# First two blocks on shared x tiles, the sums inside the token projections, the fourth block's low weights on VectorE, and the meta tokens' operations ahead of the chunk operations

## The chip, the cores and the metric

One NeuronCore of one Trainium2 chip runs the whole program. The metric is device time in microseconds; the kernel before takes 1088.43 us (median of three runs, 1088.21 to 1089.88).

## The reference

One decoder layer over 528 tokens: 16 learned meta tokens ahead of 512 real ones, model width 1024. Eight heads of width 128 run a gated delta rule; a short gated convolution runs beside it; both are merged by sigmoid gates, projected, and followed by a SwiGLU network of width 2816 and a last RMSNorm.

```
xn = rms_norm(h, norm1)
q, k, v, z, b_raw, a_raw, sc_c, sc_u, sc_b, gate_a, gate_b = split_columns(xn @ w_in, PROJ_WIDTHS)
q, k, v = silu(causal_depthwise_conv(q, k, v)), q and k L2-normalised per head
beta = sigmoid(b_raw);  g = -exp(a_log) * softplus(a_raw + dt_bias)
o = chunk_gated_delta_rule(q, k, v, g, beta)    # the meta tokens form their own first partial chunk
y_a = (rms_norm(o, o_norm) * silu(z)) @ w_dn_out
y_b = (sc_b * causal_depthwise_conv(sc_c * sc_u, conv_sc)) @ w_sc_out
h = h + (sigmoid(gate_a) * y_a + sigmoid(gate_b) * y_b) @ w_o
gt, up = split(rms_norm(h, norm2) @ w_gate_up)
h = h + (silu(gt) * up) @ w_down;  return rms_norm(h, final_norm)[:, 16:]
```

In each chunk the delta rule solves a triangular system (a_mat + I); the kernel inverts that matrix level by level, blocks of 1, 2, 4 up to 64, for the four chunks of 128 real tokens (am, tm, um) and in small for the chunk of 16 meta tokens (ma, mt, mu).

## The kernel before, in words

**Blocks.** All matrix products are cut into blocks of 128 output channels. The list BLOCKS holds for each head q, k, v, z, c, u, b, then the gates and output projections, then the SwiGLU network; block n is the n-th of the list, counted from 0. A block is eight tiles k of 128 input channels. Each weight block is 512 KB, comes by DMA on SP's queue into one of three slots of w_raw, and is split in two parts whose products are exact enough together: the high part w_hi (ScalarE, split_weights, half a block at a time, counted by whi_ready) and the low part w_lo, the difference (POOL, split_weights, counted by wlo_ready; for the first three blocks VectorE, first_low_weights, counted by wlo_first). x is split the same way (x_hi on ScalarE in plain_high, x_lo on VectorE in plain_low). Every tile then takes three products on TensorE: w_hi x_hi, w_hi x_lo, w_lo x_hi; a block over 528 or 516 tokens does each in two halves (big[n % 2]).

**The start.** first_blocks does blocks 0 and 1 (q and k of head 0) in two passes: a high pass with x_hi, block after block, and a low pass with x_lo. Meanwhile ScalarE squares the x tiles (square), VectorE adds them (add_square), and TensorE sums them over partitions with a matrix of ones; from that ScalarE makes the inverse root rs1, by which the results of all projections are scaled later. Then come token_projections (beta and decay inputs, 32 matmuls into dbank[0:2], signalled by bat_done), whose copy is turned inside block 2 (turn_token_projections), token_sums behind block 2, and turn_decays in block 3. token_factors and token_decays are the ScalarE and VectorE sides of these. ScalarE's functions Silu and Exp/Ln lie in different tables, and changing between them is an instruction of its own (ACT_TABLE_LOAD).

**Order on each engine.** Every engine runs its own list in program order, written out by hand: a loop over blocks n and quarters q of a block. In it each engine takes one step of the generator delta_steps (from block 4 on, four steps a block, 28 steps a head, so steps 0 to 3 of a head lie in its block b and steps 4 to 7 in the next head's block q), a piece of evacuate for the block before, and a weight split. TensorE takes a step after every second tile. An engine that waits holds all that stands behind it in its list.

**Steps 0 to 4 of a head.** TensorE, step 0: the products k k^T into dbank[1] (kk_done). VectorE, step 0: am, the two operations on tm, the transpose into um (u_ready). POOL, step 0: level_mask(0), then in block b both halves of the next block's low weights. VectorE, step 1: the meta operations bv, bk, ma, mkdec, mvb (ma_ready, mkv_ready), which need TensorE's mpre_done and ScalarE's mx_ready and km_root (L564). POOL, step 1: mt and the three malev (mt_ready). ScalarE, step 3: the product of level 0 copied into pb, then dbank[2] cleared (cleared), after mkv_ready. TensorE, step 3: level 0 with um and alev (L1024, um,alev). TensorE, step 4:

```
pe.wait_ge(pb_ready, done + 1)
if l == 0:
    pe.wait_ge(mt_ready, h + 1)
    if h:
        pe.wait_ge(o_root, h)
    mm(dbank[0][0:META, 0:META], mt[:, :], ident[0:META, 0:META]).then_inc(mt_turned, 1)
    pe.wait_ge(mkv_ready, h + 1)
...
if l == 0:
    pe.wait_ge(cleared, h + 1)
```

Of the kernel before, what the change touches and what calls it, by code (L numbers as in the profile page):

```python
# [65 lines left out]
def hybrid_block_kernel(nc, h_t, w_stream, w_ba, small, consts, out):  # L66
# [5 lines left out]
    with ctx:  # L72
# [196 lines left out]
        def wait_low(engine, n, half):  # L269
            if n < 3:  # L270
                engine.wait_ge(wlo_first, 2 * n + half + 1)
            else:
                engine.wait_ge(wlo_ready, 2 * (n - 3) + half + 1)
# [5 lines left out]
        def _(sp):  # L279
            sp.dma_start(sm[:, :], small[:, :]).then_inc(small_in, 16)  # L280
            for part in range(4):
                sp.dma_start(h_in[:, 2 * part:2 * part + 2, :], h_t[:, 2 * part:2 * part + 2, :]).then_inc(h_loaded[part], 16)
                if part == 0:
                    sp.dma_start(w_raw[:, 0, :], w_stream[0, :, :]).then_inc(w_in[0], 16)
            for n in range(1, STREAM):
# [20 lines left out]
        def _(pool):  # L306
# [25 lines left out]
            def delta_steps():  # L332
                for h in range(-1, HEADS + 1):
                    for step in range(0 if h >= 0 else PRE, STEPS if h < HEADS else TRAIL):
# [7 lines left out]
                        if step == 0:  # L342
                            pool.wait_ge(a_ready, h + 1)
                            level_mask(0)
                        if step == 1:
# [5 lines left out]
                            ins.then_inc(mt_ready, 1)  # L351
                        if step == 2:
# [26 lines left out]
            for n in range(STREAM + 1):  # L379
                weights_first = n < MAIN and BLOCKS[n][0] == "b"  # L380
                for q in range(4):
# [5 lines left out]
                    if q in (1, 2) and 3 <= n + 1 < STREAM and not weights_first:  # L387
# [18 lines left out]
        def _(act):  # L406
# [30 lines left out]
            split_weights(0, 0)  # L437
            split_weights(0, 1)
            for k in range(2, KT):
                plain_high(k)  # L440
            split_weights(1, 0)
            split_weights(1, 1)
            for k in range(KT):
                square(k)
            act.wait_ge(ba_in, 16)
            copy(wba_hl[:, :, 0:16], wba[:, :].rearrange("p (k c) -> p k c", c=16)).then_inc(wba_hi_ready, 1)
            split_weights(2, 0)
# [11 lines left out]
            ins.then_inc(rs1_ready, 1)  # L459
            def token_factors():  # L460
# [41 lines left out]
            def delta_steps():  # L502
                for h in range(-1, HEADS + 1):
                    nxt = h + 1
                    for step in range(0 if h >= 0 else PRE, STEPS if h < HEADS else TRAIL):
# [32 lines left out]
                        if step == 3:  # L538
# [48 lines left out]
            def evacuate(n, kind, m):  # L587
                p = big[n % 2]
                act.wait_ge(block_done, n + 1)
                if kind == "z":  # L590
# [43 lines left out]
            for n in range(STREAM + 1):  # L634
                chores = evacuate(n - 1, *BLOCKS[n - 1]) if 1 <= n <= MAIN else iter(())
                for q in range(4):
# [10 lines left out]
                    if q in (1, 2) and 3 <= n + 1 < STREAM and not weights_first and not weights_at_once:  # L647
                        split_weights(n + 1, q - 1)
                    if q == 3 and n == 2:
                        token_factors()  # L650
                    if q == (0 if n > 3 else 3) and 2 <= n and n - 2 < MAIN and BLOCKS[n - 2][0] in ("q", "k", "v"):
                        silu(*BLOCKS[n - 2])
                    if q == (0 if n < AT["gb", 0] else 2) and n in EXP_LN_FROM:
                        nc.scalar.preload_act_table_set("natural_log_exp_and_others")
                if n == 2:
# [24 lines left out]
        def _(dve):  # L680
# [26 lines left out]
            for k in range(5):  # L707
                plain_low(k)
            first_low_weights(1)
            for k in range(5, KT):  # L710
                plain_low(k)
            for k in range(1, KT):
# [3 lines left out]
                                    wba_hl[:, :, 0:16].bitcast(f32), ALU.subtract).then_inc(wba_ready, 1)  # L716
# [639 lines left out]
```

## Time and profile before

| what | value |
|---|---|
| median of the runs | 1088.43 us (1088.21, 1088.43, 1089.88) |
| profiled execution | 1087.92 us, span of its trace 1086.1 us |
| granted TensorE clock, mean | 0.995 of full speed |
| TensorE busy | 1063.2 us, 98% of the span |
| VectorE, ScalarE, POOL busy | 417.1, 423.3, 553.6 us |
| DMA | 95.44 MB, mean 88 GB/s |

The span runs from the first to the last instruction of the profiled execution; the time of that execution is 1.8 us longer. PE is TensorE's matmuls, PEld its weight loads, DVE VectorE, ACT ScalarE. A bracket behind a row tells how long the engine stood idle before it and what ended that; "issue" means that the profile shows no releaser. L1024 is the helper through which TensorE issues all its matmuls.

### The profile page before, as it was taken

What the parts mean: (1) busy time and instruction counts of PE and PEld (TensorE: products, weight loads), DVE (VectorE), ACT (ScalarE), POOL (GpSimd) and SP (SyncE); (2) the same over time, 40 slices, a digit from 0 to 9 for tenths busy, and PEclk for the clock granted to TensorE, in tenths of its full rate; (3) what the DMA queues carried; (4) which work ended last, traced back from release to release, by engine and by line L of the source; (5) the groups of instructions that cost most, each with busy time, mean ns of one, the idle gap of its engine ahead of it and who ended that gap; (6) DMA issues with size and microseconds to landing.
All of it is one profiled execution on the core that took longest, in us unless ns stands there. A gap on an engine that the chain in (4) does not pass through costs nothing.

```text
span 1086.1 us, 20289 instructions
## 1 busy us (share of the span) xinstructions
PE 1063.2 (98%) x8233; PEld 906.8 (83%) x8233; DVE 417.1 (38%) x772; ACT 423.3 (39%) x950; POOL 553.6 (51%) x471
## 2 busy tenths in 40 slices
PE   8999999999999999999999999999999999999997
PEld 8989898989898898978888888878888888888886
DVE  6665756657575657553211212212111121200001
ACT  6726354453545353533322233443322333332222
POOL 1263635364544535363545565655555555554553
PEclk9999999999999999999999999999999999999999
DMA  6221212121212121211432222222322223222222
GB/s 221 73 84 62 70 61 85 63 69 60 89 60 83 58 77 60 78 60 60 129 142 97 97 91 88 93 97 97 97 97 85 90 97 97 98 97 97 95 80 78
DMA packets 28812, 95.44 MB, mean 88 GB/s; under 512 B 2984, under 2 KB 5288, under 8 KB 28720
## 3 DMA queue, kind: packets, MB, share of 16 engines
q1 hardware_dynamic: 27520, 91.77, 25.4%
q10 hardware_dynamic: 1200, 2.38, 0.6%
q8 instruction: 65, 1.06, 0.4%
q14 instruction: 27, 0.22, 0.1%
HBM read 92.03 MB, written 2.11 MB: 87 GB/s over the span
## 4 chain that ended last, share of the span: by engine, by line
PE 96%; DVE 1%; issue 1%; ACT 1%; DMA 1%; POOL 0%; SPq 0%; DVEq 0%
PE bank L1024 95%; DMA h_in<-h_t 1%; DVE qkv L704 0%; ACT x_hi L422 0%; PE bank L1216 0%; PE bank L1222 0%; DVE x_lo L690 0%; DVE w_lo L698 0%; POOL mt L313 0%; DVE tm L767 0%; DVE h L1015 0%; PE bank L1229 0%; PE bank L1228 0%; DVE cv L929 0%; DVE am L687 0%
## 5 line engine op out<-in xcount | busy, mean ns | idle before, releaser
L326 POOL TENSOR_TENSOR w_lo<-w_raw,w_hi 128x512 fp32r<-128x512 f32 x316 | 415.6, 1332 | 477.5 <-ACT w_hi L413 476.4
L1024 PE MATMUL bank<-x_hi,w_hi 128*128 128x258 f32 (+2 forms) x896 | 249.0, 336 | 0.6 <-DVE w_lo L698 0.6
L1024 PE MATMUL bank<-x_hi,w_lo 128*128 128x258 f32 (+2 forms) x896 | 231.0, 316 | 0.0
L1024 PE MATMUL bank<-x_lo,w_hi 128*128 128x258 f32 (+2 forms) x896 | 228.9, 316 | 0.0
L413 ACT ACTIVATE w_hi<-w_raw 128x512 fp32r<-128x512 f32 x322 | 187.5, 618 | 92.3 <-PE bank L1024 92.2
L1024 PE MATMUL bank<-og_hi,w_hi 128*128 128x512 f32 x416 | 164.7, 396 | 0.0
L1024 PE MATMUL bank<-og_hi,w_lo 128*128 128x512 f32 x416 | 164.3, 395 | 0.0
L1024 PE MATMUL bank<-og_lo,w_hi 128*128 128x512 f32 x416 | 164.3, 395 | 0.0
L1024 PEld LDWEIGHTS bank<-x_hi,w_lo 128*128 128x128 f32 x896 | 148.2, 190 | 11.3
L1024 PEld LDWEIGHTS bank<-x_hi,w_hi 128*128 128x128 f32 x896 | 146.9, 190 | 12.8 <-DVE w_lo L698 0.8
L1024 PEld LDWEIGHTS bank<-x_lo,w_hi 128*128 128x128 f32 x896 | 147.2, 190 | 8.9
L1024 PEld LDWEIGHTS bank<-og_hi,w_hi 128*128 128x128 f32 x416 | 78.0, 187 | 19.2 <-issue 0.2
L1024 PEld LDWEIGHTS bank<-og_lo,w_hi 128*128 128x128 f32 x416 | 78.0, 187 | 19.2 <-issue 0.2
L1024 PEld LDWEIGHTS bank<-og_hi,w_lo 128*128 128x128 f32 x416 | 78.0, 187 | 19.2
L858 DVE SCALAR_TENSOR_TENSOR cv<-raw,sm,cv 128x528 f32<-128x528 f32 (+1 forms) x72 | 72.2, 1002 | 1.5
L1024 PE MATMUL bank<-f_hi,w_hi 128*128 128x512 f32 (+1 forms) x182 | 68.9, 378 | 0.0
L1024 PE MATMUL bank<-f_hi,w_lo 128*128 128x512 f32 (+1 forms) x182 | 68.7, 377 | 0.0
L1024 PE MATMUL bank<-f_lo,w_hi 128*128 128x512 f32 (+1 forms) x182 | 68.6, 377 | 0.0
L687 DVE TENSOR_TENSOR tg<-bank,rs 128x512 f32<-128x512 f32 x22 | 15.2, 692 | 110.1 <-PE bank L1024 101.7
L1024 PE MATMUL bank<-yb_hi,w_hi 128*128 128x512 f32 x128 | 51.6, 403 | 0.0
L1024 PE MATMUL bank<-yb_lo,w_hi 128*128 128x512 f32 x128 | 50.5, 395 | 0.0
L1024 PE MATMUL bank<-yb_hi,w_lo 128*128 128x512 f32 x128 | 50.5, 395 | 0.0
(261 smaller groups left out, 1300.5 us busy)
## 6 DMA issues: line engine op xcount, KB each, us to landing
w_raw<-w_stream SPq DMA_DIRECT2D x162, 512.0 KB, 3.3
h_in<-h_t SPq DMA_DIRECT2D x4, 528.0 KB, 5.9
h<-h_t ACTq DMA_DIRECT2D x1, 2048.0 KB, 10.9
h_in<-gc_dram SPq DMA_DIRECT2D x7, 264.0 KB, 3.1
out<-h SPq DMA_DIRECT2D x4, 256.0 KB, 2.9
out<-h SPq DMA_DIRECT2D x2, 384.0 KB, 2.6
cst<-consts SPq DMA_DIRECT2D x1, 512.0 KB, 8.3
h_in<-gc_dram ACTq DMA_DIRECT2D x1, 264.0 KB, 3.0
```

The lines of the kernel that those rows point to most:

```text
L326: nc.gpsimd.tensor_tensor(low_weights(n)[:, at], w_raw[:, n % 3, at], high_weights(n)[:, at].bitcast(f32), ALU.subtract).then_inc(wlo_read ...
L413: return nc.scalar.activation(to, x, ACT.Copy)
L687: return nc.vector.tensor_tensor(to, a, b, ALU.mult)
L858: ins = nc.vector.scalar_tensor_tensor(to, xj, taps[:, j:j + 1], to, ALU.mult, ALU.add)
L1024: return nc.tensor.matmul(o, w, x, start=start, stop=stop)
```

## The change

- SP asks for the second block's weights ahead of the second part of x; ScalarE and VectorE split them ahead of x tiles 2 to 7.
- The high pass of the first two blocks runs tile by tile, both blocks on each, after tiles 0 and 1 of the first and then of the second.
- ScalarE and VectorE handle four squares, then wba, then the other four; TensorE's sums of squares move from before the token projections to the middle of them.
- Block 3's low weights go from POOL to VectorE, its high ones ahead of the third block on ScalarE. In head 0 the last tap of the convolutions of q, k and v (a scaled copy of raw) goes from VectorE to ScalarE's evacuate, token_factors on ScalarE from the end of the third block's loop round to the end of the second's, and VectorE copies the token projections ahead of the first convolution.
- Per head, VectorE's and POOL's meta operations go from step 1 to the front of step 0, and ScalarE's clear of dbank[2] from step 3 to step 1.

```diff
--- before.py
+++ after.py
@@ -267,10 +267,10 @@
         def wait_low(engine, n, half):
-            if n < 3:
+            if n < 4:
                 engine.wait_ge(wlo_first, 2 * n + half + 1)
             else:
-                engine.wait_ge(wlo_ready, 2 * (n - 3) + half + 1)
+                engine.wait_ge(wlo_ready, 2 * (n - 4) + half + 1)
         def wait_gate_used(engine, i):
@@ -281,8 +281,9 @@
                 if part == 0:
-                    sp.dma_start(w_raw[:, 0, :], w_stream[0, :, :]).then_inc(w_in[0], 16)
-            for n in range(1, STREAM):
+                    for n in range(2):
+                        sp.dma_start(w_raw[:, n, :], w_stream[n, :, :]).then_inc(w_in[n], 16)
+            for n in range(2, STREAM):
                 if n == 2:
@@ -340,15 +341,14 @@
                         if step == 0:
-                            pool.wait_ge(a_ready, h + 1)
-                            level_mask(0)
-                        if step == 1:
                             pool.wait_ge(ma_ready, h + 1)
...
                             ins.then_inc(mt_ready, 1)
+                            pool.wait_ge(a_ready, h + 1)
+                            level_mask(0)
                         if step == 2:
@@ -384,7 +384,7 @@
                         next(delta, None)
-                    if q in (1, 2) and 3 <= n + 1 < STREAM and not weights_first:
+                    if q in (1, 2) and 4 <= n + 1 < STREAM and not weights_first:
                         split_weights(n + 1, q - 1)
@@ -434,16 +434,17 @@
             plain_high(1)
-            split_weights(0, 0)
-            split_weights(0, 1)
+            for n in range(2):
+                split_weights(n, 0)
+                split_weights(n, 1)
             for k in range(2, KT):
                 plain_high(k)
-            split_weights(1, 0)
-            split_weights(1, 1)
-            for k in range(KT):
+            for k in range(4):
                 square(k)
...
             copy(wba_hl[:, :, 0:16], wba[:, :].rearrange("p (k c) -> p k c", c=16)).then_inc(wba_hi_ready, 1)
+            for k in range(4, KT):
+                square(k)
             split_weights(2, 0)
@@ -457,6 +458,8 @@
             ins.then_inc(rs1_ready, 1)
+            split_weights(3, 0)
+            split_weights(3, 1)
             def token_factors():
@@ -535,7 +538,7 @@
                             ins.then_inc(pb_ready, 1)
-                        if step == 3:
+                        if step == 1:
                             act.wait_ge(mkv_ready, h + 1)
@@ -587,6 +590,12 @@
                 act.wait_ge(block_done, n + 1)
+                if kind in ("q", "k", "v") and m == 0:
+                    i = ("q", "k", "v").index(kind)
+                    c, first, last = conv_number(kind, 0), META if kind == "q" else 0, CQKV + 4 * 8 * i + 3
+                    act.wait_ge(raw_scaled, i + 1)
+                    nc.scalar.activation(cv[:, c % 2, first:], raw[:, c % 2, 3 + first:], ACT.Copy,
+                                         scale=sm[:, last:last + 1]).then_inc(raw_ready, 1)
                 if kind == "z":
@@ -644,14 +653,14 @@
                     next(chores, None)
-                    if q in (1, 2) and 3 <= n + 1 < STREAM and not weights_first and not weights_at_once:
+                    if q in (1, 2) and 4 <= n + 1 < STREAM and not weights_first and not weights_at_once:
                         split_weights(n + 1, q - 1)
-                    if q == 3 and n == 2:
-                        token_factors()
                     if q == (0 if n > 3 else 3) and 2 <= n and n - 2 < MAIN and BLOCKS[n - 2][0] in ("q", "k", "v"):
...
                         nc.scalar.preload_act_table_set("natural_log_exp_and_others")
+                if n == 1:
+                    token_factors()
                 if n == 2:
@@ -704,16 +713,16 @@
             first_low_weights(0)
-            for k in range(5):
+            first_low_weights(1)
+            for k in range(KT):
                 plain_low(k)
-            first_low_weights(1)
-            for k in range(5, KT):
-                plain_low(k)
-            for k in range(1, KT):
+            for k in range(1, 4):
                 add_square(k)
...
                                     wba_hl[:, :, 0:16].bitcast(f32), ALU.subtract).then_inc(wba_ready, 1)
+            for k in range(4, KT):
+                add_square(k)
             link(nc.vector.tensor_scalar(on_scaled[:, :], sm[:, ONORM:ONORM + 1], float(128) ** 0.5, None, ALU.mult))
@@ -757,17 +766,6 @@
                         if step == 0:
-                            dve.wait_ge(kk_done, h + 1)
-                            dve.wait_ge(xb_ready, h + 1)
-                            mult(flat(am), dbank[1][:, :], flat(am)).then_inc(a_ready, 1)
-                            dve.wait_ge(a_ready, h + 1)
-                            dve.wait_ge(tm_set, h + 1)
-                            t = cols4(tm[:, :, :], 1, 0)
-                            link(mult(t, cols4(am[:, :, :], 1, 0), const_cols(cst[:, CLEV, :], 1, 0)))
-                            nc.vector.tensor_tensor(t, const_cols(ident, 1, 0), t, ALU.subtract).then_inc(t_ready, 1)
-                            dve.wait_ge(t_ready, h + 1)
-                            nc.vector.transpose(flat(um), flat(tm)).then_inc(u_ready, 1)
-                        if step == 1:
                             dve.wait_ge(mpre_done, h + 1)
@@ -779,6 +777,16 @@
                                                     ALU.mult).then_inc(mkv_ready, 1)
+                            dve.wait_ge(kk_done, h + 1)
+                            dve.wait_ge(xb_ready, h + 1)
+                            mult(flat(am), dbank[1][:, :], flat(am)).then_inc(a_ready, 1)
+                            dve.wait_ge(a_ready, h + 1)
+                            dve.wait_ge(tm_set, h + 1)
+                            t = cols4(tm[:, :, :], 1, 0)
+                            link(mult(t, cols4(am[:, :, :], 1, 0), const_cols(cst[:, CLEV, :], 1, 0)))
+                            nc.vector.tensor_tensor(t, const_cols(ident, 1, 0), t, ALU.subtract).then_inc(t_ready, 1)
+                            dve.wait_ge(t_ready, h + 1)
+                            nc.vector.transpose(flat(um), flat(tm)).then_inc(u_ready, 1)
                         if step == 11:
@@ -880,22 +888,15 @@
                     if c == 0:
-                        nc.vector.tensor_scalar(cv[:, 0, META:], raw[:, 0, 3 + META:], sm[:, last:last + 1], None,
-                                                ALU.mult).then_inc(raw_ready, 1)
-                        dve.wait_ge(raw_ready, 1)
-                        taps = convolve(0, META, sm[:, CQKV + 4 * m:CQKV + 4 * m + 4])
-                        next(taps)
                         dve.wait_ge(bat_done, 1)
                         for s in range(2):
-                            ins = mult(bat[:, s * HALF:(s + 1) * HALF], dbank[s][0:32, 0:HALF],
-                                       rs1[0:32, s * HALF:(s + 1) * HALF])
+                            ins = mult(bat[:, s * HALF:(s + 1) * HALF], dbank[s][0:32, 0:HALF], rs1[0:32, s * HALF:(s + 1) * HALF])
                         ins.then_inc(bat_copied, 1)
-                        yield
-                        yield from taps
-                        return
+                        first_low_weights(3)
                     first = META if kind == "q" else 0
-                    nc.vector.tensor_scalar(cv[:, c % 2, first:], raw[:, c % 2, 3 + first:], sm[:, last:last + 1], None,
-                                            ALU.mult).then_inc(raw_ready, 1)
+                    if m:
+                        nc.vector.tensor_scalar(cv[:, c % 2, first:], raw[:, c % 2, 3 + first:], sm[:, last:last + 1], None,
+                                                ALU.mult).then_inc(raw_ready, 1)
                     dve.wait_ge(raw_ready, 3 * m + i + 1)
@@ -1036,15 +1037,14 @@
                     return parts, [big[n][s][:, 0:part.stop - part.start] for s, part in enumerate(parts)]
-                for n in range(2):
+                for k, n in [(0, 0), (1, 0), (0, 1), (1, 1)] + [(k, n) for k in range(2, KT) for n in range(2)]:
                     parts, to = outs(n)
-                    for k in range(KT):
-                        if k % 4 == 0:
-                            wait_low(pe, n, k // 4)
-                        pe.wait_ge(xhi_ready, k + 1)
-                        for w in (w_hi, w_lo):
-                            for o, s in zip(to, parts):
-                                mm(o, w[:, n, k * 128:(k + 1) * 128], x_hi[:, k, s], start=k == 0 and w is w_hi, stop=False)
+                    if k % 4 == 0:
+                        wait_low(pe, n, k // 4)
+                    pe.wait_ge(xhi_ready, k + 1)
+                    for w in (w_hi, w_lo):
+                        for o, s in zip(to, parts):
+                            mm(o, w[:, n, k * 128:(k + 1) * 128], x_hi[:, k, s], start=k == 0 and w is w_hi, stop=False)
                 for n in range(2):
@@ -1052,6 +1052,7 @@
                     ins.then_inc(block_done, 1)
+            def x_square_sums():
                 pe.wait_ge(x_added, KT - 1)
@@ -1063,6 +1064,8 @@
                                      start=k == 0 and rows == 32, stop=k == KT - 1 and rows == 32)
+                    if k == KT // 2 - 1:
+                        x_square_sums()
                 ins.then_inc(bat_done, 1)
...
```

## Rows read from the trace of the kernel before

**Rows 1.** The page: busy us, share of the span, instructions.
```profile
PE 1063.2 (98%) x8233; PEld 906.8 (83%) x8233; DVE 417.1 (38%) x772; ACT 423.3 (39%) x950; POOL 553.6 (51%) x471
```

**Rows 2.** TensorE's waits: total us, times, longest.
```profile
PE bank L1024 <- issue: 10.6, 8, 1.5
...
PE bank L1024 <- POOL malev L313: 1.4, 1, 1.4
```

**Rows 3.** All engines in order of time, second head, 112 to 122 us.
```profile
112.02 0.19 ACT L564 ACTIVATE h_in<-h_in 16x1 f32<-16x1 f32 x1
...
113.46 0.69 DVE L687 TENSOR_TENSOR am<-bank,am 128x512 f32<-128x512 f32 x1 [1.43 <-PE bank L1024]
...
114.23 1.09 POOL L313 TENSOR_TENSOR alev<-am,cst 128x256 f32<-128x256 f32 x1 [4.15 <-DVE am L687]
...
114.64 0.96 DVE L767 TENSOR_TENSOR tm<-cst,tm 128x256 f32<-128x256 f32 x1
...
115.28 1.49 POOL L326 TENSOR_TENSOR w_lo<-w_raw,w_hi 128x512 fp32r<-128x512 f32 x1
...
115.64 0.71 DVE L769 STREAM_TRANSPOSE um<-tm 128x512 f32<-128x512 f32 x1
...
117.68 0.40 PE L1024 MATMUL bank<-x_hi,w_lo 128*128 128x512 f32 x1
...
118.00 0.44 PE L1024 MATMUL bank<-um,alev 32*32 32x16 f32 x32
...
118.38 0.51 PE L1024 MATMUL bank<-x_hi,w_hi 128*128 128x258 f32 x2
118.52 0.41 ACT L413 ACTIVATE h_in<-bank 128x256 f32<-128x256 f32 x1 [1.33 <-PE bank L1024]
...
118.97 1.18 POOL L313 TENSOR_TENSOR mt<-ma,cst 16x16 f32<-16x16 f32 x1 [0.41 <-DVE ma L777]
119.07 0.33 DVE L780 TENSOR_SCALAR mvb<-bank,h_in 16x128 f32<-16x128 f32 x1
...
119.69 0.40 PE L1024 MATMUL bank<-x_hi,w_lo 128*128 128x258 f32 x2
...
120.89 0.57 POOL L313 TENSOR_TENSOR malev<-ma,cst 16x16 f32<-16x16 f32 x3
...
121.56 0.20 PE L1024 MATMUL bank<-cst,mt 16*16 16x16 f32 x2 [1.47 <-issue]
```

**Rows 4.** The chain that ended last: start us, us, what.
```profile
179.32 37.20 PE bank L1024 x492
...
238.37 35.82 PE bank L1024 x492
```

**Rows 5.** Windows of 4 us: busy by engine, PEclk, DMA share, GB/s.
```profile
core 0: us, PE busy (x) PEld busy (x) DVE busy (x) ACT busy (x) POOL busy (x), PEclk, DMA share, GB/s
180.00:184.00 4.00, 4.00 (x52) 3.73 (x53) 1.67 (x3) 0.56 (x3) 2.52 (x3) 0.58 0.02 4
412.00:416.00 4.00, 4.00 (x52) 3.73 (x53) 1.67 (x3) 0.65 (x3) 2.53 (x3) 0.57 0.01 4
```

**Rows 6.** TensorE in order of time, 0 to 45 us.
```profile
7.81 0.51 PE L1024 MATMUL bank<-x_hi,w_hi 128*128 128x258 f32 x2
...
13.04 0.51 PE L1024 MATMUL bank<-x_hi,w_hi 128*128 128x264 f32 x2 [0.58 <-DVE w_lo L698]
...
17.04 4.03 PE L1024 MATMUL bank<-x_lo,w_hi 128*128 128x258 f32 x32
...
26.02 0.41 PE L1024 MATMUL bank<-x_hi,w_hi 128*128 128x264 f32 x2
...
28.63 1.25 PE L1024 MATMUL bank<-pair,xt 32*128 32x16 f32 x10 [0.26 <-issue]
```

**Rows 7.** ScalarE in order of time, 0 to 60 us.
```profile
31.25 1.28 ACT L632 ACT_TABLE_LOAD   x1
...
35.11 1.14 ACT L413 ACTIVATE w_hi<-w_raw 128x512 fp32r<-128x512 f32 x2
```

**Rows 8.** VectorE in order of time, 0 to 60 us.
```profile
23.93 0.76 DVE L687 TENSOR_TENSOR raw<-bank,rs_mem 128x258 f32<-128x258 f32 x2 [1.14 <-issue]
...
31.92 0.76 DVE L687 TENSOR_TENSOR raw<-bank,rs_mem 128x264 f32<-128x264 f32 x2
```

## The prediction, made before the result was known

> **What bounds the kernel now.** I read the page's busy times first, then the waits of TensorE, then all engines around the longest wait, and last the first 45 us. TensorE is busy for 98% of the span [rows 1], so only three things can shorten this kernel: time in which TensorE stands still, time in which its clock is low, and the start. The view of waits puts nearly all of the standing time into one kind: eight waits, 10.6 us, ended by "issue", and one of 1.4 us ended by POOL's malev [rows 2]. One of the eight is a 0.26 us one in the start [rows 6], so the others are seven, each near 1.5 us: together with the 1.4 us one that is one for each of the eight heads.
>
> What is that wait? The engines around it in the second head answer it [rows 3]. TensorE issues its last projection pair at 119.69 and then nothing until 121.56, when the pair that turns mt goes out (L1024, cst,mt): that instruction waits for mt_ready. POOL's three malev products end at 120.89 + 0.57 = 121.46 and signal it, 0.10 before. So "issue" is here only a label for want of a matched event; the releaser is POOL, as in the head where the view names it. POOL is late because its meta operations begin at 118.97, once VectorE has written ma, and VectorE writes ma only after step 0 (am, tm, the transpose) and the chores of block "u". What ma needs was there long before: its last input, km_root, comes from ScalarE at 112.02 + 0.19 = 112.21, and VectorE then idles until 113.46, POOL until 114.23 (idle 4.15) [rows 3].
>
> There is a second cost behind it. After two of these waits the granted clock is 0.58 and 0.57 of full speed over 4 us [rows 5]; TensorE had been nearly continuously busy at full speed before the pause, so it fell from 2.4 to 1.2 GHz for most of such a stretch. The same run of 492 matmuls takes 37.20 us in a head with the fall and 35.82 us in one without [rows 4]: 1.38 us for each fall.
>
> **The meta operations (VectorE, POOL, ScalarE steps 0 and 1).** Nothing is added or removed, only the order. Without the wait the mt pair would follow at the usual distance at a change of tile size: 118.00 − 117.68 = 0.32 where the 512-column matmuls follow each other at about 0.23, so about 0.09 extra; the pair at 119.69 takes 0.24, and the mt pair would start near 119.69 + 0.33 = 120.02 instead of 121.56. That is 1.53 us a head.
>
> Is it free? New times in the second head, from [rows 3]:
> - VectorE: km_root 112.21, then five small instructions (mvb is one, 0.33 each at most), so ma near 112.9 and the last of them between 113.4 and 113.9. kk_done lets am start at 113.46 now; it is delayed by 0 to 0.4.
> - POOL: from ma_ready its five operations took 118.97 to 121.46 = 2.49, with VectorE's SBUF operations beside them. At the same price they now end near 115.4; the level mask (1.09) ends at 116.5 and the low weights of the next q block (1.49) at 118.0. TensorE wants these low weights at 118.38. So the cover is 0.4 us even at the full price; if POOL ran 1 us later the new stall would be 0.6 a head.
> - ScalarE: the clear waits for mkv_ready (113.4 to 113.9), and behind it stand the two weight copies and the inverse root; the root waits for TensorE's step 1 sums, which come after kk_done (113.4), and the first weight copy is not wanted by POOL before 116.5.
> - TensorE step 3 at 118.00 waits for u_ready, now 115.64 + 0.71 = 116.35. The delay of am (0.4) and one POOL operation in the way of each of the two tm operations bring it to at most about 117.5.
> - The other waits of step 4: pb is ready at 118.52 + 0.41 = 118.93, ahead of 120.02 by 1.1.
> So I take the whole 1.53: 8 x 1.53 = 12.2 us. Bounds: 0.9 a head if POOL comes 1 us late (7.3), and 12.4.
>
> How POOL and VectorE disturb each other is seen in one place: VectorE's tm subtraction takes 0.96 for 256 columns while POOL's level mask runs beside it, and am on 512 columns with one input from PSUM takes 0.69 alone [rows 3]. The Trainium skill (SBUF — State Buffer, "SBUF: two separate sides") says that the port pair which the two share is an exclusive lock: a VectorE operation with two SBUF inputs and a POOL operation fully block each other. It speaks against putting POOL's meta operations beside VectorE's step 0: by it each tm operation could wait for one short POOL operation (0.2 for a malev, estimate from a third of 0.57), some 0.4 us in all, and the sum would stay as it is. The trace agrees with the lock in that 0.96.
>
> **The clock.** If the pauses of 1.5 us go, what precedes the two falls goes: 2 x 1.38 = 2.8 us. Bounds: 0 and 2.8 in the profiled execution. The other executions may have one more or one fewer; the runs' median is 0.5 us above the profiled one, which a fraction of one fall would be.
>
> **The first 45 us.** *Shared x tiles.* Now the first block starts at 7.81 and is held back by ScalarE's x tiles, and the second starts at 13.04 after 0.58 of waiting [rows 6]. From the low pass, 32 matmuls take 4.03, 0.126 each. The 64 matmuls of the high pass need 8.1; with a pair of blocks on each tile TensorE needs 1.0 us a tile and ScalarE's tiles come faster. Against that, the second block's weights now go ahead of the second part of x (0.5 MB more in front of it on SP's queue, then two more copies on ScalarE and two subtractions on VectorE): I allow 0.25 of waiting. The high pass ends near 16.0 and not 17.04, the low pass near 20.0 and not 21.07: −1.1. *Sums.* The projections, 32 matmuls, are 4.03 and ended at 26.02, so the sums lay in front of them at 21.2 to 22.0. Now they come after half of them: 20.0 + 2.0 = 22.0, 0.8 later. All that hangs on them moves: VectorE's scaling of the first block ended at 23.93 + 0.76 = 24.69 [rows 8], which becomes 25.5, while TensorE is done with projections and sums at 24.8. The third block waits 0.7 and starts at 25.5 and not 26.02: −0.5. *Token projections copied before the first convolution.* The 0.26 before the turn at 28.63 goes: −0.8 in all. *Raw scaling on ScalarE.* The scaling of k waits there for VectorE (31.92 + 0.76 = 32.68), and the silu of q stands behind it with its table load, which could start at 31.25 before [rows 7, 8]. So everything behind it on ScalarE is about 2 us later: the token decays, on them VectorE's scaling of v, on that ScalarE's scaling of v and only then the fifth block's weights, whose copy began at 35.11 [rows 7]; it comes to some 38.5. The first half is 0.6 on ScalarE [rows 7] and up to 1.49 on POOL [rows 3], so 40.5; TensorE wants it near 40.1 (estimate: 25.5, then 48 pairs of matmuls at 0.24, and about 3 for the turns and sums among them, of which one turn is 1.25 [rows 6]): 0.4 is lost there, and about as much again at the sixth block, while ScalarE catches up. *The fourth block's low weights* on VectorE stand ahead of the first convolution, from which one operation of a like size has gone to ScalarE; I take the two as equal. Sum of the start: −1.1 + 0.6 − 0.3 + 0.4 + 0.3 = −0.1, taken as −0.2. Bounds: −1.5, if the chain on ScalarE costs nothing, and +1.5, if it costs twice as much.
>
> **Sum.** The profiled execution took 1087.92, its span 1086.1 and 1.8 around it. 1087.92 − 12.2 − 2.8 − 0.2 = 1072.7; that execution lies 0.5 below the median of the runs shown (1088.43), and I keep the sum as the prediction. What this kernel's measurement can tell from no change is about 0.2%, 2.2 us.
>
> **Rivals.**
> - *POOL becomes late for the q block's low weights* (or VectorE for u_ready), because the meta operations now stand ahead of them. For it: only 0.4 us of cover on POOL. Against it: the price used is already the disturbed one. At 1 us late, 0.6 x 8 = 5: 1078. Chance 0.13.
> - *The clock still falls* somewhere, after shorter pauses. For it: the start has new short ones. Against it: nothing of 1.5 us is left. 1072.7 + 2.8 = 1075.5. Chance 0.07.
> - *The start loses*: ScalarE's later chain delays the first head too. 1072.7 + 1.7 = 1074.4. Chance 0.12.
> - *The pause is not POOL's*: the label "issue" is right, and it is TensorE's own. Then it all stays: 1087.7. Against it: 0.10 us between malev's end and the start. Chance 0.03.
> - *Slower*: VectorE's step 0 is blocked at its head by the meta operations' inputs, so that u_ready comes late and step 3 of all heads stalls. It decides from a loss of 15.2 / 8 = 1.9 us a head, that is u_ready 3.5 us later than now. With a pause of 1.5 and a fall of 1.38 at each of eight heads, in place of the old ones: 1072.7 + 23 = 1096. Against it: km_root is there 1.25 before kk_done. Chance 0.02.
> - *As forecast*: 0.63, with its own range of 1071.2 to 1074.2.
>
> The range goes to the late-POOL case above and to the start's best bound with margin below: 1070.5 to 1078. Faster 0.96, within 0.2% 0.02, slower 0.02.
>
> **What would show it.** POOL's mt operations start near 1.0 us after km_root and end before the level mask; the mt pair starts 0.33 after the projection pair before it in all eight heads; no stretch under full clock before the tail; head to head 56.1 us and not 57.7 (238.37 − 179.32 − 1.38 [rows 4]). In the start: sums near 22.0, third block near 25.5, and a wait on w_lo at the fifth or sixth block. The prediction is wrong if the pair after step 3 waits for w_lo, if the mt pair waits for another event (pb, o_root, cleared), or if ScalarE's delay reaches the first head's step 0.

## The result: 1073.3 us, 1.4% faster

| | before | after |
|---|---|---|
| median of the runs | 1088.32 us (1087.21 to 1089.88, 4 runs) | 1073.29 us (1073.05 to 1073.49, 4 runs) |
| profiled execution, span | 1087.92, 1086.1 | 1073.49, 1071.4 |
| granted clock, mean of the profiled execution | 0.995 | 0.997 |

The ratio is 0.9861, 95% interval 0.9844 to 0.9878. The forecast was 1072.7 with a range of 1070.5 to 1078.0. The page after, the line that answers to [rows 1]:

```profile
PE 1059.2 (99%) x8233; PEld 903.4 (84%) x8233; DVE 418.7 (39%) x771; ACT 426.0 (40%) x953; POOL 542.6 (51%) x469
```

TensorE's waits after, the answer to [rows 2]: us in total, times, longest.

```profile
PE bank L1025 <- ACT ones_r L413: 2.4, 1, 2.4
PE bank L1025 <- POOL w_lo L327: 1.4, 2, 1.0
PE bank L1025 <- ACT sqt L683: 1.0, 1, 1.0
PE bank L1025 <- DVE raw L696: 0.7, 2, 0.5
```

The eight pauses before the mt pair are gone from the list. What is new is 1.4 us on w_lo and 0.7 us on raw, all of it in the first 65 us. All engines around the same place in the second head, the answer to [rows 3]:

```profile
111.81 0.18 ACT L567 ACTIVATE h_in<-h_in 16x1 f32<-16x1 f32 x1
...
112.17 1.05 PE L1025 MATMUL bank<-k_odd 128*128 128x128 f32 x8
112.39 0.22 DVE L775 SCALAR_TENSOR_TENSOR ma<-bank,h_in,mx 16x16 f32<-16x16 f32 x1
112.54 0.33 DVE L777 TENSOR_SCALAR mkdec<-bank,erev 16x128 f32<-16x128 f32 x1
112.69 0.21 POOL L314 TENSOR_TENSOR mt<-ma,cst 16x16 f32<-16x16 f32 x1 [2.80 <-DVE ma L775]
112.79 0.33 DVE L778 TENSOR_SCALAR mvb<-bank,h_in 16x128 f32<-16x128 f32 x1
...
113.16 0.57 POOL L314 TENSOR_TENSOR malev<-ma,cst 16x16 f32<-16x16 f32 x3
...
113.25 0.69 DVE L696 TENSOR_TENSOR am<-bank,am 128x512 f32<-128x512 f32 x1
...
114.03 1.10 POOL L314 TENSOR_TENSOR alev<-am,cst 128x256 f32<-128x256 f32 x1 [0.29 <-DVE am L696]
...
115.08 1.49 POOL L327 TENSOR_TENSOR w_lo<-w_raw,w_hi 128x512 fp32r<-128x512 f32 x1
...
118.32 0.41 ACT L413 ACTIVATE h_in<-bank 128x256 f32<-128x256 f32 x1 [1.32 <-PE bank L1025]
...
119.49 0.40 PE L1025 MATMUL bank<-x_hi,w_lo 128*128 128x258 f32 x2
...
119.82 0.18 PE L1025 MATMUL bank<-cst,mt 16*16 16x16 f32 x1
...
119.89 0.40 PE L1025 MATMUL bank<-h_in,tm 32*32 32x16 f32 x29
...
120.22 0.52 PE L1025 MATMUL bank<-x_hi,w_hi 128*128 128x258 f32 x2
```

Read it from the top. km_root ends at 111.99, ma follows at 112.39, and POOL's first mt operation at 112.69, 7.1 us ahead of the mt pair. It takes 0.21 there; it took 1.18 in [rows 3]. The three malev end at 113.73. am starts at 113.25, behind TensorE's k k^T products (k_odd, done at 113.22) and not behind mvb, which ends 0.10 before them at 113.12: the meta operations do not delay it in this head. The mt pair goes out at 119.82, 0.33 after the projection pair of 119.49, and the next projections at 120.22. The level mask (114.03) and the low weights (115.08) stand where they stood, with the same durations, once the 0.20 by which this head is early in the trace is added.

The chain that ended last, of the second and third heads after (start, us, what), the answer to [rows 4]:

```profile
107.70 47.84 PE bank L1025 x595
...
163.75 47.79 PE bank L1025 x597
```

The window behind the mt pair after, the answer to [rows 5], with the same columns:

```profile
120.00:124.00 4.00, 4.00 (x99) 3.67 (x92) 1.97 (x4) 1.69 (x6) 2.67 (x3) 1.00 0.29 114
```

A head is now 163.75 − 107.70 = 56.05 us, and the clock is at full speed in that window as in all windows of 4 us between the start and the tail. TensorE in the start after, the answer to [rows 6]:

```profile
8.29 0.49 PE L1025 MATMUL bank<-x_hi,w_hi 128*128 128x258 f32 x2
...
21.91 1.05 PE L1025 MATMUL bank<-qkv,ones_mem 128*128 128x264 f32 x4
...
25.38 0.51 PE L1025 MATMUL bank<-x_hi,w_hi 128*128 128x264 f32 x2 [0.48 <-DVE raw L696]
...
27.78 1.28 PE L1025 MATMUL bank<-pair,xt 32*128 32x16 f32 x10
...
40.62 0.48 PE L1025 MATMUL bank<-x_hi,w_hi 128*128 128x258 f32 x2 [0.40 <-POOL w_lo L327]
...
48.06 0.48 PE L1025 MATMUL bank<-x_hi,w_hi 128*128 128x258 f32 x2 [0.98 <-POOL w_lo L327]
...
61.55 0.44 PE L1025 MATMUL bank<-um,alev 32*32 32x16 f32 x32
62.20 0.51 PE L1025 MATMUL bank<-x_hi,w_hi 128*128 128x258 f32 x2 [0.21 <-DVE raw L696]
```

ScalarE there, the answer to [rows 7]:

```profile
32.02 0.74 ACT L597 ACTIVATE cv<-raw,sm 128x528 f32<-128x528 f32 x1 [1.54 <-DVE raw L696]
32.77 1.28 ACT L641 ACT_TABLE_LOAD   x1
...
38.33 1.14 ACT L413 ACTIVATE w_hi<-w_raw 128x512 fp32r<-128x512 f32 x2
```

ScalarE waits 1.54 us for VectorE's raw before it can copy k, and only behind that come the table load (32.77, before at 31.25) and, by way of the token decays, the fifth block's weights (38.33, before at 35.11).

The third block starts at 25.38 (26.02 before) and the turn at 27.78 (28.63 before). Then two waits for POOL's w_lo, 0.40 at the fifth block and 0.98 at the sixth, turn the 0.85 us of lead into a lag: TensorE's step 3 of head 0 (um,alev) stands at 61.55 after and at 60.40 before, and a wait of 0.21 for raw follows.

### The profile page after: what moved, and what is told of

It reads as the page before. It is cut to its first block, busy times and chain, and to the rows that moved or that the text cites. A ratio compares the mean times of both kernels' runs of the same rounds, so it can differ in the third digit from the quotient of the medians.

```text
span 1071.4 us, 20292 instructions
## 1 busy us (share of the span) xinstructions
PE 1059.2 (99%) x8233; PEld 903.4 (84%) x8233; DVE 418.7 (39%) x771; ACT 426.0 (40%) x953; POOL 542.6 (51%) x469
## 4 chain that ended last, share of the span: by engine, by line
PE 95%; DVE 2%; ACT 1%; issue 1%; DMA 0%; DVEq 0%; ACTq 0%
PE bank L1025 95%; DVE cv L866 1%; DMA h_in<-gc_dram 0%; PE bank L1225 0%; PE bank L1219 0%; DVE raw L696 0%; ACT cv L597 0%; DVE am L696 0%; ACT L661 0%; ACT L476 0%; ACT L641 0%; ACT L417 0%; ACT qkv L641 0%; DVE w_lo L707 0%; DVE xt L696 0%
```

## The experiments

Eleven kernels ran, all on one core. Kernels of one group ran on the same chip with shared runs of the kernel before.

**1. Only the meta operations' order.**

```diff
-                        if step == 0:                          # VectorE
-                            dve.wait_ge(kk_done, h + 1)
...
-                        if step == 1:
+                        if step == 0:
                             dve.wait_ge(mpre_done, h + 1)
...
+                            dve.wait_ge(kk_done, h + 1)
...
-                        if step == 1:                          # POOL
+                        if step == 0:
                             pool.wait_ge(ma_ready, h + 1)
...
+                            pool.wait_ge(a_ready, h + 1)
+                            level_mask(0)
...
-                        if step == 3:                          # ScalarE
+                        if step == 1:
                             act.wait_ge(mkv_ready, h + 1)
```

> The kernel before with only the order of the meta operations changed (VectorE, POOL, ScalarE's clear), the start as before. Theory 1 (the whole gain is the pause before the mt pair and the clock falls behind it, and the changed start is a loss): 8 pauses of 1.5 to 1.65 and on average two falls of 1.4 go, 1088.3 - 13 - 2.8 = 1072.5, and since the changed start seems to cost about 1 us, this is up to 1.5 us faster than the changed kernel: 1071.8 to 1072.5. Theory 2 (the start gains, as its parts were meant to): slower than the changed kernel, 1073.5 to 1075. Both expect no stretch under full clock before the tail.

Measured: 1072.39 us (1072.13 to 1072.56), ratio 0.9853, interval 0.9838 to 0.9868. That is 0.9 faster than the changed kernel, though in another group of runs; the spans of the two traces differ by 1.1 (1070.3 and 1071.4). TensorE in its start:

```profile
13.38 0.51 PE L1022 MATMUL bank<-x_hi,w_hi 128*128 128x264 f32 x2 [0.60 <-DVE w_lo L697]
...
28.96 1.25 PE L1022 MATMUL bank<-pair,xt 32*128 32x16 f32 x10 [0.25 <-issue]
...
60.72 0.44 PE L1022 MATMUL bank<-um,alev 32*32 32x16 f32 x32
```

It keeps the 0.6 us wait at the second block, and still its step 3 of head 0 is at 60.72, where the changed kernel has 61.55 with the same first product (8.33 and 8.29). The whole gain, and 0.9 us more, is in this part. The kernel before had its first product at 7.81 in its trace; the other traces of this study with 16 warming matmuls lie between 8.08 and 8.79, so 0.3 of the lag at head 0 against that one trace is chance.

**2. Only the start.**

The base is the changed kernel; the edits of experiment 1 are taken back on all three engines.

```diff
-                        if step == 1:                          # ScalarE, and so on
+                        if step == 3:
                             act.wait_ge(mkv_ready, h + 1)
```

> The changed kernel with the meta operations back in their old order. Theory 1: the pauses and one to three clock falls are back, and the changed start costs about 1: 1088.8 to 1090. Theory 2: the start gains about 1: 1087 to 1087.5. A third: the start has no effect and the pauses are not what was removed: 1073.

Measured: 1089.37 us (1088.83 to 1090.83, 11 runs) against 1088.61 for the kernel before; ratio 1.0011, interval 1.0002 to 1.0020. Its waits on TensorE:

```profile
PE bank L1027 <- issue: 10.3, 7, 1.5
...
PE bank L1027 <- POOL w_lo L327: 1.4, 2, 1.0
```

The seven and one pauses are back, and so are the 1.4 us on w_lo. The eleven times fall in two groups with nothing between: six from 1088.83 to 1089.37, with a mean clock of 0.994 or 0.995, and five from 1090.53 to 1090.83, with 0.993. The medians of the two groups lie 1.8 apart, near the price of one fall of the clock (1.38). That the executions of the second group had one more fall fits this and the mean clocks; only one execution has a trace, so it is not shown. The traced execution (1088.96) has two falls, as the one of the kernel before has (1087.92): between these two the changed start costs 1.0. The falls stand behind other pauses, though, the second and the sixth of the eight here and the third and the seventh before; what picks them is open.

**3. Only VectorE's part of it.**

The base is the kernel before. POOL's mt and malev stay at step 1, behind both halves of the next block's low weights, and ScalarE's clear at step 3.

```diff
-                        if step == 1:                          # VectorE
+                        if step == 0:
                             dve.wait_ge(mpre_done, h + 1)
...
+                            dve.wait_ge(kk_done, h + 1)
```

> The kernel before with only VectorE's meta operations moved ahead of am; POOL's mt and malev stay behind the q block's low weights, ScalarE's clear at step 3. Theory 1 (POOL's place matters too): POOL starts mt when its low weights end, near 118.6 in the second head, and needs 1.0 to 2.5 us beside VectorE's two convolution taps, so that the mt pair waits 0 to 1 us in each head and the clock seldom falls: 1074 to 1080. Theory 2 (ma was all that POOL waited for): as the meta-only kernel, 1072.5.

Measured: 1077.77 us (1077.54 to 1078.08), ratio 0.9902, interval 0.9889 to 0.9916. All engines in the second head:

```profile
116.97 1.28 POOL L326 TENSOR_TENSOR w_lo<-w_raw,w_hi 128x512 fp32r<-128x512 f32 x1 [0.50 <-ACT w_hi L413]
...
117.51 1.28 DVE L936 SCALAR_TENSOR_TENSOR cv<-raw,sm,cv 128x512 f32<-128x512 f32 x1
...
118.21 0.66 POOL L313 TENSOR_TENSOR mt<-ma,cst 16x16 f32<-16x16 f32 x1
...
118.83 0.75 DVE L940 SCALAR_TENSOR_TENSOR cv<-raw,sm,cv 128x512 f32<-128x512 f32 x1
...
118.95 0.71 POOL L348 TENSOR_TENSOR mt<-cst,mt 16x16 f32<-16x16 f32 x1
...
119.63 0.57 POOL L313 TENSOR_TENSOR malev<-ma,cst 16x16 f32<-16x16 f32 x3
...
120.30 0.20 PE L1023 MATMUL bank<-cst,mt 16*16 16x16 f32 x2 [0.51 <-issue]
```

ma is early here, but POOL starts mt only behind its low weights, and from there it and VectorE's two convolution taps take turns: the tap of 117.51 takes 1.28, where the other takes 0.75, beside low weights that end at 118.25; mt (0.66) and the subtraction on it (0.71) each end just behind a tap (118.79, 119.58). malev ends at 120.20 and the mt pair goes out at 120.30 after a pause of 0.51. There are eight such pauses, none is followed by a low clock, and the time lies 4.5 to 5.4 above the two kernels without pause: POOL's place is worth about a third of the gain. ScalarE's clear at step 3 was done at 118.91 and held nothing.

**4. The last tap of k and v back on VectorE.** The base is the changed kernel.

```diff
-                if kind in ("q", "k", "v") and m == 0:
+                if kind == "q" and m == 0:
...
-                    if m:
+                    if m or kind != "q":
                         nc.vector.tensor_scalar(cv[:, c % 2, first:], raw[:, c % 2, 3 + first:], ...
```

> The changed kernel with the last tap of k and v of head 0 back on VectorE (q's stays on ScalarE). Theory 1 (ScalarE's wait for VectorE ahead of the silu of q delays the fifth and sixth blocks' weights): the waits of 0.4 and 1.0 us on w_lo at 40.6 and 48.1 go, or nearly, 1073.3 - 1.3 = 1072.0. Theory 2 (they are late for another reason, VectorE's extra low weights or the table loads): they stay, 1073.3.

Measured: 1071.63 us (1071.21 to 1071.96), ratio 0.9845, interval 0.9832 to 0.9859. TensorE in the start:

```profile
49.16 0.60 PE L1225 MATMUL bank<-cst,qkv 128*128 128x128 f32 x4
...
59.61 0.44 PE L1025 MATMUL bank<-um,alev 32*32 32x16 f32 x32
```

No wait on w_lo is left. The turn of the token projections is at 27.82 as in the changed kernel (27.78), the transposes in the sixth block at 49.16 (51.03 there, the row is not shown) and step 3 of head 0 at 59.61, 1.94 earlier than there. So the two idle times of 0.40 and 0.98 cost 1.9 in the flow of products: the idle time of a row counts only from the modelled end of the last product, while the next would have been issued before that end. Row by row, the lead of this kernel grows by 0.65 over the first of them and by 1.27 over the second.

**5. The sums of squares after two tiles.** The base is kernel 4.

```diff
-                    if k == KT // 2 - 1:
+                    if k == 1:
                         x_square_sums()
```

> The version with k and v back on VectorE, and TensorE's sums of squares after two tiles of the token projections in place of four. Theory 1 (the third block waits for the inverse root): the squares are added by 20.66, the second tile ends near 20.95, so the sums come 1.0 earlier, the root with them, and the 0.48 wait ahead of the third block at 25.4 goes: 1071.6 - 0.5 = 1071.1. Theory 2 (the wait's place is taken by the squares, which are not added in time, or by the copy of the token projections): 1071.6.

Measured: 1070.72 us (1070.58 to 1070.97), ratio 0.9836, interval 0.9822 to 0.9849. TensorE's turn of the projections in it:

```profile
27.28 1.28 PE L1025 MATMUL bank<-pair,xt 32*128 32x16 f32 x10
```

TensorE in kernel 4, the same stretch:

```profile
21.96 1.05 PE L1025 MATMUL bank<-qkv,ones_mem 128*128 128x264 f32 x4
...
25.43 0.51 PE L1025 MATMUL bank<-x_hi,w_hi 128*128 128x264 f32 x2 [0.48 <-DVE raw L696]
...
27.82 1.28 PE L1025 MATMUL bank<-pair,xt 32*128 32x16 f32 x10
```

The 0.48 wait of 25.43 is gone and the turn is 0.54 earlier. In the times the difference to kernel 4 is 0.9, but between two groups of runs; the traces' 0.5 is the better figure.

**6. The high pass block after block again.** The base is kernel 4; the second block's DMA and its high and low weights are in their old places too.

```diff
-                for k, n in [(0, 0), (1, 0), (0, 1), (1, 1)] + [(k, n) for k in range(2, KT) for n in range(2)]:
+                for n in range(2):
+                    for k in range(KT):
```

> The version with k and v back on VectorE, and the high pass again block after block, the second block's weights and low weights back in their old places. Theory 1 (sharing the tiles gains its 1.1 at the end of the low pass, and the root's lateness only takes part of it): low pass ends near 21.1 to 21.4 and the third block starts about 1 later, 1072.6. Theory 2 (the gain is lost again in the wait for the root): 1071.7.

Measured: 1072.58 us (1072.42 to 1072.76), ratio 0.9853, interval 0.9839 to 0.9866. TensorE:

```profile
22.91 1.05 PE L1027 MATMUL bank<-qkv,ones_mem 128*128 128x264 f32 x4
...
26.39 0.51 PE L1027 MATMUL bank<-x_hi,w_hi 128*128 128x264 f32 x2 [0.48 <-DVE raw L696]
```

The sums are at 22.91 and not 21.96, and the third block, still 0.48 behind the root, starts at 26.39 and not 25.43. Sharing the tiles is worth 0.96 us, and all of it arrives.

**7. A longer pause.** The base is the kernel before.

```diff
+                            for _ in range(5):
+                                link(mult(malev[:, 0, :], ma[:, :], cst[0:META, CLEV + 1, 0:META]))
                             for l in range(META_LEVELS):
                                 ins = mult(malev[:, l, :], ma[:, :], cst[0:META, CLEV + 1 + l, 0:META])
```

> The kernel before with five more 16x16 products on POOL in front of malev in each head (the same product written again), so that the pause is about 2.9 us and not 1.5. Theory 1 (the fall of the clock hangs on the pause, and a longer one is followed by a fall more often): 8 x 1.4 = 11.2 for the pauses and up to six more falls of 1.4: 1104 to 1108. Theory 2 (falls as often as before): 1099.8. Theory 3 (something else holds TensorE at that place): less than 1099.

Measured: 1115.24 us (1112.48 to 1116.31), ratio 1.0241, interval 1.0225 to 1.0257, more than any of the theories gave. Its chain that ended last, at one head (start, us, what):

```profile
370.56 2.91 issue
373.48 38.17 PE bank L1026 x496
```

Its windows behind that pause (the granted clock is the third number from the end):

```profile
374.00:378.00 4.00, 4.00 (x65) 3.70 (x58) 1.71 (x3) 0.16 (x2) 2.68 (x4) 0.50 0.00 0
378.00:382.00 4.00, 4.00 (x60) 3.77 (x59) 1.36 (x5) 2.35 (x6) 2.62 (x3) 0.84 0.02 4
```

The pause is 2.91 and the clock is low behind all eight of them. The same stretch of about 495 matmuls then takes 38.17, against 35.82 in [rows 4] without a fall and 37.20 with the fall behind a pause of 1.5. So a fall costs 2.35 here and not 1.38, which the theory had not foreseen; over the eight heads it is 2.3 to 2.7, 19.4 in all. 8 x (2.92 − 1.47) = 11.6, plus 19.4 − 2 x 1.38 = 16.6, makes 28.2; the profiled execution took 1116.31 − 1087.92 = 28.4 more.

**8. ScalarE's clear back at step 3.** The base is the changed kernel.

```diff
-                        if step == 1:
+                        if step == 3:
                             act.wait_ge(mkv_ready, h + 1)
```

> The changed kernel with ScalarE's clear of dbank[2] back at step 3. Theory 1 (the clear is ready near 119.1, ahead of the mt pair at 119.8, and its move does nothing): 1073.3. Theory 2 (it is the next wait): a pause of up to 0.5 in each head, 1075 to 1077.

Measured: 1073.44 us (1073.23 to 1073.57), ratio 0.9860. The move of the clear does nothing that can be measured.

**9 to 11. The rest of the start.** The base is kernel 5: the fourth block's low weights back on POOL; the last tap of q on VectorE as well; 12 warming matmuls.

```diff
-            if n < 4:                                          # low3_on_pool, in wait_low
+            if n < 3:
...
-                        first_low_weights(3)
```

```diff
-                if kind == "q" and m == 0:                     # q_on_vector, in ScalarE's evacuate
```

```diff
-WARM = 16
+WARM = 12
```

> The version with k and v on VectorE and the sums after two tiles, and the fourth block's low weights again on POOL. Theory 1 (POOL is idle there, and nothing of TensorE waits for these weights in either place): the same within 0.3, 1070.7. Theory 2 (VectorE's first convolution, slowed by POOL beside it, makes the decay inputs late for token_sums at 32.3): 1071.2 to 1072.

> The same version with the last tap of q on VectorE too, so that none of the three is on ScalarE. Theory 1 (q's, for which ScalarE has time before token_factors, neither helps nor harms): 1070.7. Theory 2 (it keeps VectorE 0.5 earlier with the decay inputs, and TensorE waits for them without it): 1071.2.

> The same version with 12 warming matmuls in place of 16. In the traces the first product starts at 7.81 to 8.33, partly when the warming ends and partly when the first low weights are there. Theory 1 (the warming holds it in some executions): 0 to 0.3 faster, 1070.5. Theory 2 (fewer of them leave the clock low at the first products): slower, 1071 to 1073.

Measured: 1070.45 (1070.34 to 1070.74), 1070.58 (1070.30 to 1070.99) and 1070.68 us (1070.56 to 1070.75), ratios 0.9832, 0.9833 and 0.9833, each with an interval of about 0.0014 to either side. None can be told from kernel 5: neither VectorE's low weights for the fourth block nor q's tap on ScalarE contributes to the change. Of warm_12 the expectation of a gain of up to 0.3 is not met; its first product starts at 7.96 but waits there for w_lo.

Kernel 5 and its three variants beat both kernels of this study: 1070.5 to 1070.7, some 2.7 us or 0.25% below the changed one.

## Why the forecast held

- **What the pause was.** Right: POOL's mt_ready, not "issue". Shown by the changed order alone (experiment 1) and by more POOL work in the same place (experiment 7): the pause grew by 1.45, the eight products there took 2.01 where the three took 0.57. In the trace before, the mt pair starts 0.09 to 0.14 behind the last malev in all eight heads.
- **Its price.** Forecast 1.53 a head, 12.2 in all. Measured: heads without a fall took 57.67 (238.37 − 179.32 − 1.38, [rows 4]) and take 56.05, so 1.62 a head, 13.0 in all. What the term left out is behind the pause: before, the mt pair went out 0.2 ahead of the tm products and the next projections came 0.58 behind it; after, it is issued among them and the next projections come 0.40 behind it (119.82, 120.22). Of these 0.18 the head as a whole keeps 0.08.
- **That it is free on POOL and VectorE.** Right, with more room than I gave it: I charged POOL 2.49 for its five operations, their price beside VectorE's taps; in the new place they take 1.04, and the first starts 0.70 behind km_root (forecast 1.0). So the rival of a late POOL, at 0.13, had less for it than the forecast said: its low weights start at 115.08 as if nothing had been put before them. Experiment 3 shows the mechanism of that rival, in the place where the taps are.
- **The two engines' lock.** The same 16x16 product on POOL takes 0.21 beside VectorE's mkdec and mvb, which read PSUM, and 1.18 in [rows 3], where the first convolution tap (119.33, 0.73 long, a row not shown) reads SBUF: it ends at 120.15, 0.09 behind that tap. In experiment 3 mt and the subtraction end 0.08 behind a tap each. By the Trainium skill (SBUF — State Buffer, "SBUF: two separate sides") whichever of the two starts first holds the shared port pair for its whole instruction, and the other fully blocks. The traces agree with the block, not with the order as recorded: the mt of 118.97 starts 0.36 ahead of the tap and still ends behind it. I gave the rule as one that speaks against the change; it speaks for it, since the old place was the one with the collision.
- **The clock.** Right: no fall in the profiled execution after, and 2 x 1.38 = 2.8 of the gain. The spread of the times says the same of the others: 1087.2 to 1089.9 before, 1073.05 to 1073.49 after. The reason given holds in what could be tried: pauses of 0.51, none of eight followed by a fall; of 1.47, two of eight (in two kernels); of 2.91, eight of eight. Why six pauses of 1.47 had no fall behind them is not known.
- **The start.** Its steps were near: sums at 21.91 (forecast 22.0), third block at 25.38 (25.5), the waits at the fifth block 0.40 (0.4) and the sixth 0.98 ("about as much again"). The sum of them was the mis-sized term: its parts add to −0.1, it was put at −0.2, and it came out at +1.0. In the two traces step 3 of head 0 is 1.15 later and a wait of 0.21 follows, +1.36; 0.32 of it is the chance of the start from one execution to the next (60.72 with the same old start in experiment 1), so the change costs 1.0. What I had too small is ScalarE's chain: the sum allowed 0.7 for the waits at the fifth and sixth blocks, and they cost 1.9. ScalarE did not catch up; it reached head 0's km_root at 56.30 and not 54.37 (54.80 in experiment 1), 1.5 to 1.9 late. This is a sign that the forecast itself had named as proof of being wrong, ScalarE's delay reaching the first head's step 0, and it came true: VectorE's meta operations, now ahead of am, hold am there until 57.84, where experiment 2 has it at 57.41 right behind TensorE, and raw and the next projections come 0.2 late. In experiment 2, with the same start and the old order, that last wait is missing, so it takes both parts of the change. Experiment 4 shows the cause of the rest: without k and v on ScalarE all these waits but the 0.48 of the third block are gone.
- **The sum.** −13.0 − 2.8 + 1.4 = −14.4, and the spans differ by 14.7. The errors of the two terms, 0.8 more gain and 1.6 less, partly cancel. That 1072.7 stood so near to 1073.3 is in part luck: with the start as it came out and the pauses at their forecast price the sum would have been 1074.3.

- **The other rivals.** That the pause is not POOL's, and that the clock still falls, are refuted above. The slower outcome, a step 0 that blocks, did not come about: the gain of 1.62 a head has no room for it, and only head 0 has a trace of it, 0.2. That the start loses (chance 0.12, by ScalarE's later chain delaying the first head) is what happened, by that mechanism, at 1.0 and not 1.5. The chances hold one slip: a pause that is not POOL's has 0.03 and would end at 1087.7, within 0.2% of the kernel before, but "within 0.2%" has only 0.02.

That a part with several good steps lost time as a whole was within the stated bounds (+1.5) but not what I expected. It is split thus, from the traces: shared tiles −0.96 (experiment 6); sums in the middle and token projections copied early −0.2 together (the turn is 1.18 ahead of experiment 1's, 28.96, less the tiles); k and v on ScalarE +1.9, and the wait on raw +0.2 (experiment 4). That makes +0.9, against 1.0 measured. The earlier place of token_factors was not tried by itself. Going two tiles earlier with the sums gains 0.5 more (experiment 5).

## What to carry to other kernels

A wait labelled "issue" very likely has a releaser if it ends at the same distance behind one instruction each time (here 0.1); look at what stands in that instruction's own queue before blaming the engine that waits. Small operations whose inputs are ready early should stand ahead of the long ones on each engine of the chain, not only on the first: moving VectorE's alone left a third of the gain unrealised. And a task moved to a seldom busy engine is only cheap if it doesn't wait there: ScalarE's copies took 0.7 us each, but each waited for VectorE with a table load and the next weights behind it.

## What the runs showed of the hardware

- The price of a fall of TensorE's clock is not one number. Behind a pause of 1.47 it cost 1.38 us, in two heads of eight; behind one of 2.91 it cost 2.3 to 2.7, in eight of eight. The lower of the two levels behind each is 1.2 GHz: windows of 1 us there show 0.50 of full speed.
- A 16x16 product on POOL takes 0.21 us beside VectorE operations that read PSUM, and 0.66 to 1.18 beside its convolution taps from SBUF, where it ends just behind the end of a tap. For such small operations the place in time matters more than their size.
